# A Mamba-2 and mixture-of-experts layer on one core: the order of its opening, from the input's load to the first group of heads

## The reference

```
shift, scale, gate, ... = split(silu(c) @ ada_w + ada_b, 6)      # six rows of 1024
h = x * (1 + scale) + shift                                      # 512 x 1024
z, xbc, dt = split(h @ w_in, [2048, 2048 + 3072])                # dt: 32 heads
xbc = silu(causal conv of 4 taps over time + bias)               # -> xs (2048), B (512), C (512)
dt = softplus(dt + dt_bias);  a = -exp(a_log)
y  = chunked scan of the state space (decays from cumsum(dt * a), B, C, xs) + d_skip * xs
y  = rms_norm(y * silu(z)) * norm_g;  x1 = layer_norm(ALPHA * x + gate * (y @ w_out))
then a mixture of 16 SwiGLU experts, top 2 of one group of 4, and a second layer norm
```

## Time and profile before

| | us |
|---|---|
| three timed runs | 1121.5, 1122.24, 1126.23; median 1122.24 |
| the profiled execution, its own time | 1123.46 |
| its span, first to last instruction | 1121.7 |
| busy PE, DVE, ACT, POOL in the span | 1037.4, 898.5, 612.1, 513.6 |
| mean granted TensorE clock | 0.988 |

### The profile page before, as it was taken

The page is one execution under the profiler, slowest core; times in us unless marked ns, Lnnn a source line. Parts: engine busy times, 40 slices in busy tenths (PEclk is TensorE's granted clock), DMA queues, the critical chain, the costliest instruction groups (busy, mean ns, idle before and its releaser), DMA issues.

```text
span 1121.7 us, 15075 instructions
## 1 busy us (share of the span) xinstructions
PE 1037.4 (92%) x4954; PEld 817.8 (73%) x4954; DVE 898.5 (80%) x958; ACT 612.1 (55%) x595; POOL 513.6 (46%) x327
## 2 busy tenths in 40 slices
PE   0778999989999997999999999999999999999996
PEld 0557778868877886874588878778787887777873
DVE  6695994896599367882698988988898999898997
ACT  1344463356246335450476676767676766676760
POOL 1333654555465445104334574245522763356455
PEclk9997999999999998999999999999999999999999
DMA  9226523532352345676599999999999999999993
GB/s 353 82 78 225 162 84 94 168 112 86 120 164 79 94 133 189 263 255 242 190 340 367 345 363 354 354 363 377 349 348 363 376 371 329 350 365 349 359 367 131
DMA packets 99597, 283.08 MB, mean 252 GB/s; under 512 B 9848, under 2 KB 50976, under 8 KB 82159
## 3 DMA queue, kind: packets, MB, share of 16 engines
q1 hardware_dynamic: 92922, 270.65, 67.1%
q0 software_dynamic: 5264, 11.86, 2.9%
q10 hardware_dynamic: 1382, 0.21, 0.1%
HBM read 274.51 MB, written 15.73 MB: 259 GB/s over the span
## 4 chain that ended last, share of the span: by engine, by line
DMA 21%; PE 20%; DVE 15%; ACT 6%; issue 6%; POOL 1%; DVEq 0%; SPq 0%; ACTq 0%; POOLq 0%
DMA moe<-in_moe_w_up 11%; DVE moe_r L1281 10%; DMA moe<-in_moe_w_down 9%; ACT moe_r L880 6%; PE ps L1859 3%; DVE moe L1386 1%; PE ps L1530 1%; PE ps L1532 1%; PE ps L1531 1%; PE ps L1611 1%; PE ps L1838 1%; PE ps L1842 1%; PE ps L1840 1%; DVE moe_r L1378 1%; DVE moe_r L1392 1%
## 5 line engine op out<-in xcount | busy, mean ns | idle before, releaser
L1281 DVE TENSOR_TENSOR moe_r<-moe,moe_r 128x2048 fp32r<-128x2048 f32 x180 | 417.8, 2337 | 72.7 <-ACT moe_r L880 71.9
L880 ACT ACTIVATE moe_r<-moe 128x2048 fp32r<-128x2048 f32 x180 | 345.6, 1926 | 162.5 <-DMA moe<-in_moe_w_up 97.3
L1838 PE MATMUL ps<-moe_r 128*128 128x512 f32 x720 | 212.9, 400 | 5.9 <-DVE moe_r L1281 5.5
L1840 PE MATMUL ps<-moe_r 128*128 128x512 f32 x720 | 205.9, 390 | 0.0
L1842 PE MATMUL ps<-moe_r 128*128 128x512 f32 x720 | 205.6, 390 | 0.0
L549 POOL TENSOR_TENSOR ssd_r<-ssd,ssd_r 128x1024 fp32r<-128x1024 f32 x56 | 138.2, 2469 | 126.3 <-ACT ssd_r L703 121.6
L1838 PEld LDWEIGHTS ps<-moe_r 128*128 128x128 f32 x720 | 130.6, 188 | 38.2 <-DVE moe_r L1281 13.8
L1840 PEld LDWEIGHTS ps<-moe_r 128*128 128x128 f32 x720 | 135.2, 188 | 29.2
L1842 PEld LDWEIGHTS ps<-moe_r 128*128 128x128 f32 x720 | 135.2, 188 | 29.1
L630 POOL DMA_INDIRECT ydram<-moe,moe_i x14 | 30.4, 2172 | 243.3 <-DVE moe L1398 243.3
L1530 PE MATMUL ps<-ssd_r 128*128 128x512 f32 x320 | 130.3, 407 | 7.0 <-DVE ssd L1024 5.3
(11 more groups left out here) (297 smaller groups left out, 1534.6 us busy)
## 6 DMA issues: line engine op xcount, KB each, us to landing
moe<-in_moe_w_up SPq DMA_DIRECT2D x116, 1024.0 KB, 6.9
moe<-in_moe_w_down SPq DMA_DIRECT2D x64, 1024.0 KB, 7.6
ssd<-in_ssd_w_in SPq DMA_DIRECT2D x40, 512.0 KB, 4.0
...
```

Source lines behind the costliest of these rows:

```text
L880: act.activation(wr[:, part_slot(i), 0, :], ring[:, i % RING, :], ACT.Identity).then_inc(s_wh, 1)
L1281: dve.tensor_tensor(wr[:, part_slot(i), 1, :], ring[:, i % RING, :], wr[:, part_slot(i), 0, :].bitcast(F32), ALU.subtract).then_inc(s_wl, 1)
L1838: mm(to[i], xh, wh[i], start=start, stop=False)
L1840: mm(to[i], xh, wl[i], start=False, stop=False)
```

## The change

x is loaded ahead of the `ada_w` pieces, and the eighth piece comes as two halves of columns, each half holding the columns of shift and scale for four chunks; DVE accumulates it in two operations. The small copies move ahead of the eight accumulations on DVE, and PE no longer waits for them before it turns chunks 0 to 5. The column sums are made in four pairs of chunks; DVE copies each pair's four sums from PSUM to a tile `modc` ahead of the scaling. Unit 0 of the weights is split between chunks 4 and 6 on ACT and POOL. DVE's taps are put ahead of parts of the step chain, PE does all six tiles before the products for `elast` and `tok`, the masked copies of `acg` take four operations over 64 rows and two for a split in place of 8 over 32 rows, and ACT's exponential of `elast` comes last in the opening. In every `turn`, PE enters on two of the six silus, does the broadcast rows of heads 0 and 1 before it turns x, and DVE's copy of `elast` goes behind the weighting of x.

```
-        mod_bank = lambda k: 0 if k < 4 else 7
+        mod_bank = lambda p: (0, 7)[p % 2]
+        column_half = lambda a, n: a.rearrange("p (a h n) -> p a h n", a=2, h=2)[:, :, n, :]
...
-                sp.dma_start(adaA[k], adaA_v[:, k, 0:2 * D]).then_inc(ld_adaA[k], 16)
+                if k < DC - 1:
+                    sp.dma_start(adaA[k], adaA_v[:, k, 0:2 * D]).then_inc(ld_adaA[k], 16)
+                else:
+                    for n in range(2):
+                        sp.dma_start(column_half(adaA[k], n), column_half(adaA_v[:, k, 0:2 * D], n)).then_inc((ld_adaA[k], ld_ada[1])[n], 16)
                 if k == 0:
                     sp.wait_ge(s_acc0, 2)
                     sp.dma_start(accA[0:1, :], ada_b[0:1, 0:2 * D]).then_inc(ld_b0, 16)
-                if k == DC - 3:
-                    for t in range(TT):
-                        sp.dma_start(oacc[:, t, :], x[0, t * P:(t + 1) * P, :]).then_inc(ld_x, 16)
...
-            unit_low(0, 0)
+                if k == 4:
+                    unit_low(0, 0)
...
-            unit_high(0, 0, 1)
+                if k == 4:
+                    unit_high(0, 0, 1)
...
+            silu(0, 0)
+            silu(0, 1)
+            conv0(0, 2)
+            unit_high(4, 0, 3)
             act.wait_ge(s_pre, 10)
             act.activation(dtv[1][0:32], dtv[1][0:32], ACT.Exp).then_inc(s_prea, 1)
-            silu(0, 0)
-            silu(0, 1)
-            for i in range(2, 4):
-                conv0(0, i)
-                unit_high(i + 2, i % 2, 3)
+            conv0(0, 3)
+            unit_high(5, 1, 3)
             silu(0, 2)
-            act.wait_ge(s_tokp, 1)
-            act.activation(elast, ps[:, 4, 0:P].rearrange("p (j n) -> p j n", j=HG), ACT.Exp).then_inc(s_el, 1)
-            silu(0, 3)
             conv0(0, 4)
             turn_unit(0, 0)
+            silu(0, 3)
             conv0(0, 5)
             silu(0, 4)
             silu(0, 5)
+            act.wait_ge(s_tok, 2)
+            act.activation(elast, elast, ACT.Exp).then_inc(s_el, 1)
...
-            for k in range(DC):
+            dve.wait_ge(s_rowp, 3)
+            dve.tensor_copy(taps, ps[:, 0, 0:120].rearrange("p (k j) -> p k j", k=5)).then_inc(s_rowc, 1)
+            dve.tensor_copy(normg32, ps[:, 0, 128:160]).then_inc(s_rowc, 1)
+            dve.tensor_copy(dskip, ps[:, 0, 192:208]).then_inc(s_rowc, 1)
+            dve.wait_ge(s_const, CONSTS)
+            dve.tensor_copy(gmask[32:64, :], gmask[0:32, :]).then_inc(s_rowc, 1)
+            for k in range(DC - 1):
                 dve.wait_ge(ld_adaA[k], 16)
                 if k:
                     dve.wait_ge(s_adaA, k)
                 dve.scalar_tensor_tensor(accA, adaA[k], cact[:, k:k + 1], accA, ALU.mult, ALU.add).then_inc(s_adaA, 1)
-            dve.wait_ge(s_rowp, 3)
-            dve.tensor_copy(taps, ps[:, 0, 0:120].rearrange("p (k j) -> p k j", k=5)).then_inc(s_rowc, 1)
-            dve.tensor_copy(normg32, ps[:, 0, 128:160]).then_inc(s_rowc, 1)
-            dve.tensor_copy(dskip, ps[:, 0, 192:208]).then_inc(s_rowc, 1)
-            modcol = lambda j: ps[:, mod_bank(j % DC), 160 + j:161 + j]
+            dve.wait_ge(s_adaA, DC - 1)
+            for n in range(2):
+                dve.wait_ge((ld_adaA[DC - 1], ld_ada[1])[n], 16)
+                half = column_half(accA, n)
+                dve.scalar_tensor_tensor(half, column_half(adaA[DC - 1], n), cact[:, DC - 1:DC], half, ALU.mult, ALU.add).then_inc(s_adaA, 1)
+            modcol = lambda k, a: modc[:, 4 * (k // 2) + 2 * a + k % 2:4 * (k // 2) + 2 * a + k % 2 + 1]
             def hin_low(k):
                 dve.wait_ge(s_hinh, k + 1)
                 dve.tensor_tensor(hin[:, 1, k, :], hraw[:, k % 4, :], hin[:, 0, k, :].bitcast(F32), ALU.subtract).then_inc(s_hinv, 1)
             for k in range(DC):
-                dve.wait_ge(s_modp, k // 4 + 1)
+                p = k // 2
+                if k % 2 == 0:
+                    dve.wait_ge(s_modp, p + 1)
+                    dve.tensor_copy(modc[:, 4 * p:4 * p + 4], ps[:, mod_bank(p), 160 + 4 * p:164 + 4 * p]).then_inc(s_rowc, 1)
+                    dve.wait_ge(s_rowc, 4 + p + 1)
...
-                dve.tensor_scalar(hraw[:, k % 4, :], bank(x_bank(k)), modcol(DC + k), modcol(k),
+                dve.tensor_scalar(hraw[:, k % 4, :], bank(x_bank(k)), modcol(k, 1), modcol(k, 0),
...
-                dve.tensor_copy(gel, elast[:, :, ds(TT * g, TT)]).then_inc(s_gc, 1)
...
-                dve.wait_ge(s_gc, 4 * g + 4)
+                dve.wait_ge(s_gc, 4 * g + 3)
...
+                dve.wait_ge(s_el, 1)
+                dve.tensor_copy(gel, elast[:, :, ds(TT * g, TT)]).then_inc(s_gc, 1)
+                dve.wait_ge(s_gc, 4 * g + 4)
...
-            dve.wait_ge(s_rowc, 3)
             xbc_taps(0)
...
+            xbc_tile(0, 0)
             step(dve.tensor_tensor(cv, cv, uv, ALU.mult))
...
-            xbc_tile(0, 0)
+            xbc_tile(0, 1)
...
-            xbc_tile(0, 1)
+            xbc_tile(0, 2)
+            split = ysplit[0:64, 0, 1, :]
+            dve.tensor_copy(split[0:32], stk[0:32]).then_inc(s_dtv, 1)
+            dve.wait_ge(s_dtv, 3)
+            dve.tensor_tensor(split[32:64], stk[0:32], split[0:32].bitcast(F32), ALU.subtract).then_inc(s_dtv, 1)
+            dve.wait_ge(s_dtv, 4)
             for g in range(G):
-                dve.tensor_scalar(acg[0:32, g, :], stk[0:32], gmask[0:32, g:g + 1], None, ALU.mult).then_inc(s_dtv, 1)
-            dve.wait_ge(s_dtv, 2 + G)
-            for g in range(G):
-                dve.scalar_tensor_tensor(acg[32:64, g, :], stk[0:32], gmask[0:32, g:g + 1], acg[0:32, g, :].bitcast(F32), ALU.mult, ALU.subtract).then_inc(s_dtv, 1)
+                dve.tensor_scalar(acg[0:64, g, :], split.bitcast(F32), gmask[0:64, g:g + 1], None, ALU.mult).then_inc(s_dtv, 1)
             dve.tensor_reduce(every8, ident.rearrange("p (a j) -> p j a", j=HG), AX.X, ALU.add).then_inc(s_dtv, 1)
-            dve.wait_ge(s_dtv, 3 + 2 * G)
+            dve.wait_ge(s_dtv, 5 + G)
             dve.tensor_copy(every8r, every8).then_inc(s_dtv, 1)
+            xbc_tile(0, 3)
             dve.wait_ge(s_prea, 5)
             step(dve.tensor_tensor(stk[64:96], ev, v, ALU.mult))
-            xbc_tile(0, 2)
-            xbc_tile(0, 3)
+            xbc_tile(0, 4)
             dve.wait_ge(s_tokp, 2)
             dve.tensor_copy(tok, ps[:, 5, 0:TT * 96].rearrange("p (c s h) -> p c s h", c=TT, s=3)).then_inc(s_tok, 1)
-            xbc_tile(0, 4)
+            dve.tensor_copy(elast, ps[:, 4, 0:P].rearrange("p (j n) -> p j n", j=HG)).then_inc(s_tok, 1)
             xbc_tile(0, 5)
-            dve.wait_ge(s_tok, 1)
-            dve.wait_ge(s_el, 1)
+            dve.wait_ge(s_tok, 2)
...
-            pe.wait_ge(s_adaA, DC)
-            for k in range(DC):
-                for j in (DC + k, k):
-                    op = mm(ps[:, mod_bank(k), 160 + j:161 + j], accA[:, j * P:(j + 1) * P], ones[:, 0:1], start=True, stop=True)
-                if k % 4 == 3:
-                    op.then_inc(s_modp, 1)
-            for k in (6, 7):
-                pe.wait_ge(s_hraw, k - 5)
-                x_chunk(k)
+            pe.wait_ge(s_rowc, 3)
+            for p in range(4):
+                if p == 0:
+                    pe.wait_ge(s_adaA, DC)
+                elif p >= 2:
+                    pe.wait_ge(s_adaA, DC + 1)
+                    pe.wait_ge(s_rowc, 4 + p - 1)
+                if p == 3:
+                    for k in (6, 7):
+                        pe.wait_ge(s_hraw, k - 5)
+                        x_chunk(k)
+                for a in range(2):
+                    for k in (2 * p, 2 * p + 1):
+                        col, j = 160 + 2 * a + k + 2 * p, a * DC + k
+                        op = mm(ps[:, mod_bank(p), col:col + 1], accA[:, j * P:(j + 1) * P], ones[:, 0:1], start=True, stop=True)
+                op.then_inc(s_modp, 1)
...
-            for i in range(4):
+            for i in range(NT):
                 xbc_tile(0, i)
-            pe.wait_ge(s_dtv, 4 + 2 * G)
+            pe.wait_ge(s_dtv, 6 + G)
...
-            xbc_tile(0, 4)
-            xbc_tile(0, 5)
...
-                pe.wait_ge(s_silu, NT * (g + 1))
+                pe.wait_ge(s_silu, NT * g + 2)
...
+                pe.wait_ge(s_oacc, 8 * g + 1)
+                acum_rows(g, 0)
+                acum_rows(g, 1)
+                pe.wait_ge(s_silu, NT * (g + 1))
                 for k in range(TT):
                     if k == 0:
                         pe.wait_ge(s_cv, NT * g + NT)
-                    if k == 1:
-                        pe.wait_ge(s_oacc, 8 * g + 1)
                     for j in range(4):
                         op = nc.tensor.transpose(ps[:, x_banks[k], j * P:(j + 1) * P], xT[:, j, k * P:(k + 1) * P], ident)
                     op.then_inc(s_xtr, 1)
-                acum_rows(g, 0)
-                acum_rows(g, 1)
...
-            pe.wait_ge(s_tok, 1)
-            pe.wait_ge(s_el, 1)
+            pe.wait_ge(s_tok, 2)
```

9 lines of the change are left out of this document (5 added, 4 removed).

## The result

The changed kernel took 1107.57 us (median of 4 runs, 1107.28 to 1110.74) against 1121.87 for the kernel before beside it (4 runs): ratio 0.9877, interval 0.9838 to 0.9916, so 14.3 us faster. Forecast were 1102 and a range of 1096 to 1111. In a later session 12 runs of the same kernel gave 1114.21 against 1119.03 (16 runs): ratio 0.9976, interval 0.9948 to 1.0005. Both are results: 14.3 us in the first session and 4.8 in the second. The second's interval holds 1, so it isn't told from no change, and its median lies outside the forecast's range.

What follows compares the result with a forecast made beforehand. PE was taken to bound the groups, with slack in the opening. Gains of 8.6 + 0.3 + 11.7 + 0.3 = 20.9 us took the profiled 1123.46 to 1102.6, or 1101.3 from the median; forecast 1102, range 1096 to 1111.

Steps and rivals of the forecast that it cites:

- A: Start to first scaling of h: 32.4 us instead of 41.01, 8.6 gained, bounds 7.0 and 9.2.
- B: First scaling to tile 0's first product: 12.0 us instead of 12.3, 0.3 gained, bounds -2.5 and +1.7.
- C: Tile 0's first product to group 0's turned x: 39.8 us instead of 51.5, 11.7 gained, bounds 6 and 13.
- D: Group 0's turned x to the first head on DVE: 5.0 us instead of 5.3, 0.3 gained.
- the groups: Groups 1 to 3: first chunk some 0.5 us later, but PE is the bound; cost 0, bounds 0 and 1.5.
- the other small edits: Opening: a copied mask and a wait counted otherwise cost a few tenths, on a DVE that waits for the pieces.
- small loads late beyond 12 us: Rival in the opening: x delays ACT's small loads, each us beyond 12 costs one; about 1106, chance 0.03.
- x first gains 1.3: Opening: x asked for first fills the transfer hole between 5 and 10 us, 1.3 us earlier, bounds 0 and 2.
- The direction of the clock: First scaling to tile 0: more dt products run at TensorE's lower clock, costing 1 us, bounds 0 and 3.
- Rival 1: DVE becomes the bound of stretch C: two to four meetings with POOL cost 5 to 7 us; about 1108, chance 0.18.
- signs of being wrong: A DVE step of 2 us or more in stretch C, half clock in tile 1, or group 0 over 99 us.
- the opening has slack and the groups have none: Whole kernel: PE busy 94.5 of 98 us in a full group, so an earlier group 0 should reach the end.

Runs made afterwards that it cites:

- e2: The changed kernel with DVE's four small copies moved behind the seventh accumulation, x still first: 1106.54 us (4 runs), ratio 0.9876 to the kernel before.
- e1: The changed kernel with x again loaded behind the sixth piece: 1107.15 us (4 runs), ratio 0.9879 to the kernel before.
- e6: e1 with dummy products on TensorE ahead of the column sums and of the third and fourth pair of sums: 1108.95 us (one run).
- e9: e1 with the edits of e3, e4 and e6, and unit 0 moved ahead of all chunks of h on ACT and POOL: 1098.02 us (one run).
- the second profile: The changed kernel itself, unchanged, profiled again in the later session: 1114.21 us (12 runs), ratio 0.9976 to the kernel before.
- e4: The changed kernel with ACT's exponential of elast one place earlier, ahead of the last silu: 1108.92 us (4 runs), ratio 0.9892 to the kernel before.
- e3: The changed kernel with TensorE's old order in every group, x turned before the broadcast rows: 1109.96 us (5 runs), ratio 0.9904 to the kernel before.

## Why the prediction was right and wrong

The time lay in the range, with the right sign. But the way there was half wrong, and it was in part luck: the profile gained 10.9 us up to the experts, where I had summed 20.9, and 5.2 in a part that I had left unchanged. By the first alone the profiled execution would have taken 1123.46 - 10.9 = 1112.6, above my range, as the second session's 1114.21 is. The 10.9 are, by stretches, 1.6 in A, -2.1 in B, 13.6 in C, -1.2 in D and -1.0 in the groups; I had 8.6, 0.3, 11.7, 0.3 and 0.

- **A, the step that failed: 8.6 forecast, 1.6 found.** It failed at "the other small edits (...) are a few tenths ahead of the pieces' landing, on a DVE that waits for them". The copies now stand ahead of the accumulation, and what they wait for comes behind 2 MB of x: 16.65, not 7.9. I had this as a rival (small loads late beyond 12 us, each us costs one) and gave it 0.03. Its price was near (16.65 less 12 is 4.7): eight accumulations from 18.55, 2.46 each, end at 38.4, 6.3 beyond my 32.1, and from there to the first scaling it is 1.0 instead of 0.3. Its chance was far too low, for the rates of the earlier trace rows spoke for it: the engines were full from 10 us on, and the small loads had used the one window that wasn't. The term "x first gains 1.3" has the wrong sign: about 1.5 lost (e2). With x behind, my own steps give 33.7; e1 has 34.04.
- **B, 12.0 forecast, 14.4 found.** My own terms give 12.3 + 2 + 1 - 2.6 = 12.7, not 12.0, so the sum should have been 20.2. The direction of the clock was right, its size 2.35 instead of 1 (6.35 against 4.0 to the first dt product, e6), inside the bounds; with the clock and unit 0's meeting both out of the way B takes 11.2 (e9). The granted clock was 0.50, the level of 1.2 GHz, from 24 us on, where PE had been idle since 21.9, through the 32 records of the column sums and up to 51.2. My reading of the profile before was off, too: there the clock was 1.00 from 34 to 42 us, right behind 25 us in which PE was idle, fell to 0.50 at 42.5 under work and was back at 45.9, so its 10 us of work aren't what had brought it up. I had also miscounted the sums: each is two records, so a pair of chunks is 8, at 0.219 rather than 0.118 (the earlier trace rows has 3.77 for 32).
- **C, 39.8 forecast, 37.8 found**, and all of the gain: 13.6, just above my bound of 13. Six tiles run without a wait in 32.7 and the clock stays at 1.00; I had 33.0 and allowed 1.5 of waits. The stretch in one window, and a full group against the earlier trace rows:
```profile
53.80:91.60 37.80, 36.10 (x171) 29.83 (x169) 29.72 (x49) 20.63 (x26) 17.33 (x9) 1.00 0.48 158
...
191.00:289.00 98.00, 94.21 (x499) 75.64 (x498) 74.13 (x111) 44.83 (x62) 50.92 (x25) 1.00 0.39 116
```
  Rival 1, DVE held up by POOL, is what the second profile shows: 5 to 7 us it said, 5.9 are found at the turned x. It had two to four meetings that cost up to 2.1 each; there are two, of 5.88 and 3.41, and the first one alone, with the clock that falls behind it, makes the loss. It isn't the alternative to my forecast but a second outcome of the same kernel, and one profile can't show both.
- **D, 5.0 forecast, 6.5 found.** I had put the exponential "beside the weightings" and priced no return of the table; both loads (1.28 each) stood ahead of the weight unit and B's copy. e4 takes 1.3 of it back.
- **Groups, 0 forecast with a bound of 1.5, about 1 found**: the turn's order costs 0.5 us a group (e3), as much as the turned x comes later, though I had argued that PE's own stream, busy 94.21 of 98 in the window above, holds the same work and so nothing would be lost.

Two of my signs of being wrong came true: a DVE step of over 2 us in stretch C (the second profile), and a group 0 of over 99 us (100.6 from turned x to turned x, 99.1 before).

What held: the opening has slack and the groups have none, so what tile 0 or the first head gains reaches the experts. Over the 13 changed profiles the stretch from the first head to the experts is 394.8 to 398.4.
